# Groups of 16 products in the first idle times of TensorE, and behind the last norm's sum

## The reference

```python
sh1, sc1, g1, sh2, sc2, g2 = _ada(c, ada_w[i], ada_b[i])
hx = _modulate(_rmsnorm(x, norm1_g[i]), sh1, sc1)
csh1, csc1, cg1, csh2, csc2, cg2 = _ada(c_ctx, ada_w[i], ada_b[i])
hc = _modulate(_rmsnorm(ctx, norm1_g[i]), csh1, csc1)
...
return _rmsnorm(x, final_norm_g)
```

## Time and profile before

| | us |
|---|---|
| median of 3 runs | 2122.95 |
| lowest, highest | 2110.27, 2126.66 |
| span of the profiled execution | 2138.7 |

### The profile page before, as it was taken

The page is one execution under the profiler, slowest core; times in us unless marked ns, Lnnn a source line. Parts: engine busy times, 40 slices in busy tenths (PEclk is TensorE's granted clock), DMA queues, the critical chain, the costliest instruction groups (busy, mean ns, idle before and its releaser), DMA issues.

```text
span 2138.7 us, 44829 instructions
## 1 busy us (share of the span) xinstructions
PE 2071.3 (97%) x17120; PEld 1995.6 (93%) x17120; DVE 1608.4 (75%) x1892; ACT 1044.1 (49%) x1489; POOL 81.8 (4%) x63
## 2 busy tenths in 40 slices
PE   6989999999999999999999999999999999999997
PEld 3678888899999999999999989999999999999997
DVE  3238989898888888988888868998886664456665
ACT  2355666545555555433455543465555553335553
POOL 0000000031000000000000211200000000000012
PEclk8999999999999999999999999999999999999999
DMA  9954666796888788899888836968865555555663
GB/s 374 364 218 161 234 219 235 264 379 232 291 293 291 278 291 286 326 371 373 314 293 290 293 110 252 356 217 287 282 233 181 186 185 190 194 194 189 195 189 128
DMA packets 127805, 547.37 MB, mean 256 GB/s; under 512 B 14576, under 2 KB 15088, under 8 KB 107120
## 3 DMA queue, kind: packets, MB, share of 16 engines
q1 hardware_dynamic: 127728, 546.31, 71.9%
HBM read 544.16 MB, written 2.10 MB: 255 GB/s over the span
## 4 chain that ended last, share of the span: by engine, by line
PE 85%; DVE 10%; ACT 2%; DMA 2%; issue 1%; SPq 0%; DVEq 0%; ACTq 0%
PE bank L1397 27%; PE bank L1398 26%; PE bank L1399 26%; DVE acc L878 3%; DVE w_lo L855 2%; DMA early<-early_w 1%; PE bank L1489 1%; PE bank L1476 1%; DVE pt_lo L859 1%; DVE negmax L1054 1%; PE bank L1403 1%; ACT prob L629 1%; PE bank L1405 1%; PE bank L1404 1%; DVE v_lo L859 0%
## 5 line engine op out<-in xcount | busy, mean ns | idle before, releaser
L496 ACT CAST w_hi<-raw 128x1024 fp32r<-128x1024 f32 x642 | 671.9, 1049 | 523.0 <-PE bank L1399 414.9
L855 DVE TENSOR_TENSOR w_lo<-raw,w_hi 128x1024 fp32r<-128x1024 f32 x642 | 787.6, 1239 | 182.8 <-ACT w_hi L496 182.5
L1397 PE MATMUL bank<-h_hi,w_hi 128*128 128x256 f32 x3216 | 899.5, 280 | 3.1 <-DVE h_lo L1182 3.1
L1398 PE MATMUL bank<-h_lo,w_hi 128*128 128x256 f32 x3216 | 898.5, 279 | 0.0
L1399 PE MATMUL bank<-h_hi,w_lo 128*128 128x256 f32 x3216 | 898.4, 279 | 0.0
L1397 PEld LDWEIGHTS bank<-h_hi,w_hi 128*128 128x128 f32 x3216 | 608.7, 189 | 6.1 <-issue 3.7
L1399 PEld LDWEIGHTS bank<-h_hi,w_lo 128*128 128x128 f32 x3216 | 608.4, 189 | 0.0
L1398 PEld LDWEIGHTS bank<-h_lo,w_hi 128*128 128x128 f32 x3216 | 604.3, 188 | 0.0
L1397 PE MATMUL bank<-a_hi,w_hi 128*128 128x256 f32 x1408 | 391.8, 278 | 2.1 <-DVE a_lo L859 2.0
L1399 PE MATMUL bank<-a_hi,w_lo 128*128 128x256 f32 x1408 | 391.2, 278 | 0.0
L1398 PE MATMUL bank<-a_lo,w_hi 128*128 128x256 f32 x1408 | 391.2, 278 | 0.0
(11 more groups left out here) (195 smaller groups left out, 2049.6 us busy)
## 6 DMA issues: line engine op xcount, KB each, us to landing
raw<-weights SPq DMA_DIRECT2D x642, 512.0 KB, 4.8
ada<-ada_late SPq DMA_DIRECT2D x160, 1024.0 KB, 5.1
early<-early_w SPq DMA_DIRECT2D x64, 512.0 KB, 7.9
ctx_s<-ctxT SPq DMA_DIRECT2D x4, 512.0 KB, 5.7
x<-xT SPq DMA_DIRECT2D x4, 512.0 KB, 8.5
outT<-h_pre SPq DMA_DIRECT2D x4, 512.0 KB, 2.6
dft_s<-dft SPq DMA_DIRECT2D x1, 1040.0 KB, 8.3
conv_s<-conv SPq DMA_DIRECT2D x2, 176.0 KB, 5.8
```

Source lines behind the costliest of these rows:

```text
L496: act.copy(w_hi[:, slot, :], raw[:, slot, :]).then_inc(hi_done, 1)
L855: dve.tensor_tensor(w_lo[:, slot, :], raw[:, slot, :], w_hi[:, slot, :].bitcast(f32), ALU.subtract)\
L1397: pe.matmul(out, wh, hi_part, start=first, stop=False)
L1398: pe.matmul(out, wh, lo_part, start=False, stop=False)
```

## The change

ScalarE rounds each piece of x into a slot of `w_hi`, behind its squares, and counts `x_rounded`. TensorE gets three helpers. `run(times, cols)` does 16 products (by default) of 256 columns: a 128x128 piece of slot 2 as stationary operand, a piece of slot 0 as moving one, into `bank[3]`, which nobody reads there. `small(n)` does n float32 products of `ident` with 4 columns and then a `run()`. `short(cols, n)` does n products of so many columns and then a `run()`. They stand behind the pairs a = 0 to 12 of the first quarter, and behind `residual_sum(3)`. No result changes.

```diff
@@ -224,7 +224,7 @@
         sq_done, sqt_done, norm_summed, var_done, std_done, rstd_done = (
             sem(n) for n in ("sq_done", "sqt_done", "norm_summed", "var_done", "std_done", "rstd_done"))
         sq0_done, lat_sq, lat_done, xr_done = sem("sq0_done"), sem("lat_sq"), sem("lat_done"), sem("xr_done")
-        eps_set = sem("eps_set")
+        eps_set, x_rounded = sem("eps_set"), sem("x_rounded")
         pre_done, h_hi_done, h_ready = sem("pre_done"), sem("h_hi_done"), sem("h_ready")
         lat_pre, lat_hi, lat_ready = sem("lat_pre"), sem("lat_hi"), sem("lat_ready")
         kr_taken, kr_rot, kr_step, kr_hi_done, kr_ready, kr_zero = (
@@ -543,6 +543,9 @@
             for n in range(2):
                 for r in range(4):
                     piece_squares(n, r)
+                    if n:
+                        act.copy(w_hi[:, r, :], x[:, QK * r:QK * r + QK, :].rearrange("p k n -> p (k n)"))\
+                            .then_inc(x_rounded, 1)
             std(1, NTOK)
             for g in range(QUARTERS):
                 rows(g)
@@ -1541,6 +1544,22 @@
                     if t % 2:
                         mm.then_inc(chunk_used, 2)
 
+            def run(times=16, cols=SEQ):
+
+                for _ in range(times):
+                    pe.matmul(bank[3][:, 0:cols], w_hi[:, 2, 16:16 + P], w_hi[:, 0, 0:cols], start=True, stop=True)
+
+            def small(n):
+
+                for t in range(n):
+                    pe.matmul(bank[3][:, 4 * t:4 * t + 4], ident, ident[:, 0:P:32], start=True, stop=True)
+                run()
+
+            def short(cols, n=1):
+
+                run(n, cols)
+                run()
+
             def rope_keys(c, half, u0=0, u1=8):
 
                 pe.wait_ge(lo_done, c + 1)
@@ -1561,6 +1580,29 @@
             for a in range(0, N_EARLY, 2):
                 g, k = a // KT, a % KT
                 early_pair(a)
+                if a == 0:
+                    pe.wait_ge(x_rounded, 4)
+                    run()
+                if a == 2:
+                    small(1)
+                    small(2)
+                if a == 4:
+                    small(4)
+                    short(128)
+                if a == 6:
+                    small(8)
+                    short(64)
+                if a == 8:
+                    small(1)
+                    short(32)
+                    short(128, 2)
+                if a == 10:
+                    small(4)
+                    short(128)
+                if a == 12:
+                    small(8)
+                    short(64)
+                    small(2)
                 if g and k == 2:
                     turn(g - 1)
                 if g and 6 <= k < 14:
```

## The result

The changed kernel took 2157.68 us (median of 4, 2146.07 to 2163.23) beside 2118.63 us for the kernel before (4 runs, 2110.27 to 2126.66). The ratio is 1.0157, with a 95% interval of 1.0117 to 1.0198: slower by 33 us, between 25 and 42. The forecast was 21.3 us, with 0.48 each for slower and for within 1%. The direction is right and the size is short by a third. The medians alone are 39 us apart (1.0184, inside the interval), and 2157.68 lies 1.7 us above the forecast range of 2131 to 2156. The ratios here leave out runs that lie more than 1.5% above the fastest of their kernel; medians, lowest and highest stand for all runs. Most of what follows is about why one change can be 33 us in one sample and 21 in the next.

What follows compares the result with a forecast made beforehand. TensorE, with work in 2071.3 of 2138.7 us, was taken as the bound. Front 22.9, give-back -2.6 and tail 1.0 make +21.3 us on 2122.95: 2144 us, 8-in-10 range 2131 to 2156.

Steps and rivals of the forecast that it cites:

- Copies at nothing: ScalarE's four roundings of x at the start add 4.0 us of its time, covered by TensorE's work: price 0.
- 15 runs at 1.83 us, 27.5 us: Groups of 16 products on TensorE ahead of pair a = 14, at full clock, no discount for the repeated operand.
- Small and short products, 8.3 us with the changes between them: In the front: 30 small products 7.5 us, seven short ones 0.6, changes of kind between runs 0.2.
- Changes of kind at the pairs, 2.1 us: In the front: six pairs between float32r products cost 0.3 us more each, two half so 0.3 together.
- Pair a = 14 at 69.1 us: First quarter's pair that sets the whole rest ends at 69.1 us in place of 46.2, 22.9 us later.
- 2.6 us given back: Behind pair a = 14, full clock and loads already landed return 2.6 us, bounds 0 and 5.3.
- Tail 1.0 us: Added products behind the last norm's sum, 12.8 us, end 1.0 us past the last store, bounds 0 and 3.
- the rival's mechanism: Clock falls to half behind each group of eight small products, twice in front, once at the end: 2149 us, chance 0.22.
- Cheaper products: Added products cost less than the profile rows: small ones at half, runs at 107 ns a product: 2137.5 us, chance 0.20.
- Not slower: Up to 190 us the stream of loads sets the pace, so the front's delay comes back: 2121 us, chance 0.05.
- Full give-back: All cold work and both load waits behind 46.2 us leave the path, 5.3 us: 2141.5 us, chance 0.08.
- Every stage from 100 to 2120 us as long as before: Sign of the forecast: past the front, no stage up to 2120 us changes its length.

Runs made afterwards that it cites:

- e5: Kernel before plus only ScalarE's four copies of x and TensorE's wait for them, no added products: 2134.47 us.
- e6: Changed kernel with only the 15 groups of 16 in the front, no small or short products, nothing behind the last sum: 2121.51 us.
- e2: The changed kernel once more, unchanged: 2143.01 us, ratio 1.0099 to the kernel before.
- e8: Changed kernel with only as many added products as the first quarter's waits hold (102), nothing behind the last sum: 2124.68 us, ratio 1.0009 to the kernel before.
- e1: The kernel before, unchanged, measured against itself: 2127.91 us, ratio 1.0011.
- e9: Kernel before plus four 512-column float32 products at two places of each layer's feed-forward: 2115.97 us, ratio 0.9954.
- e11: The kernel of e9 measured once more: 2113.58 us, ratio 0.9976 to the kernel before.
- e4: Changed kernel without the front's added products, keeping the copies and the products behind the last norm's sum: 2123.64 us, ratio 0.9997 to the kernel before.
- e10: Kernel before plus four small 4-column products at the same places as in e9: 2132.82 us, ratio 1.0035.
- e7: Changed kernel with 32 small products in place of eight at three places: 2175.61 us.

## Why the prediction was right, and where it was short

- *Copies at nothing*: right (e5).
- *15 runs at 1.83 us, 27.5 us*: a little low. In the front a step is 117 ns and not 114, so 240 products are 28.1 us (e6).
- *Small and short products, 8.3 us with the changes between them*: 8.1 (e6). *Changes of kind at the pairs, 2.1 us*: about 1.3, what is left of the whole (44.8 - 28.1 - 8.1 - 7.3).
- *Pair a = 14 at 69.1 us*: 67.9. TensorE began 0.8 us sooner, since its clock rose at 11.5 and not at 13.1 us. From the first pair on it is 44.8 us (forecast 45.2). The bet on the whole stretch was right: all of what did not fit into the gap was paid.
- *2.6 us given back*: 2.3 us; the end of pair a = 14 moved by 21.7 and VectorE's 61st instruction by 19.4. That instruction lies 0.6 us apart in before and e1, so the 2.3 is good to about that.
- *Tail 1.0 us*: 0.8 us (1.2 in e2). TensorE ended 12.3 us behind the sum (forecast 12.8).
- *Clock stays full at eight small products*: right; the rival's mechanism is shown at 32.
- *Cheaper products*: fell. *Not slower*: fell; with the DMA share at 0.62 in the front nothing came back. *Full give-back*: fell; e8 has VectorE's turned rows 1.9 us sooner and keeps 0.5 at the 61st instruction.
- *Every stage from 100 to 2120 us as long as before*: this step failed. I took the loops' times of one profile as the kernel's. In the profile of after the shift grew to 26.0 us at 1400 us and fell back to 12.3 behind the last up-projection, in code that was not touched. The steps differ from execution to execution, worth up to 12.6 + 5.0 + 13.0 us in the three loops and 3.4 in layer 1's square product. My own sign of being wrong, a later stage shorter by 10 us or more, came true with it (up 1 by 13.0), though the change is not its cause: e1, without the change, has it too.

So the mechanism and the sum are right, at 19 to 21 us by every measure that takes the draws out. What the 33 us of the result has over it I put down to the draws of four runs beside four; only one of these runs of after has a profile, so that is argued and not shown. My half per cent of scatter in medians was somewhat low (the two medians of after are 14.7 us, 0.7%, apart) and had no cause. Not settled: what decides the draw. With the 512-column products in front of the loops 21 of the 24 runs of e9 and e11 are under 2120 us, where 9 of the 46 runs of before beside them are. Why they help is open, since the step behind such products can also be the long one (e4 above). That a break of another kind does not help (e10) is one kernel and twelve runs.

## What to carry to other kernels

An engine's waits can be filled for nothing only up to their length; the rest is queued in front of the step that everything else waits for, and is paid in full. Before two profiles are compared, look at the count of products in equal stretches of untouched loops. If it differs, subtract the stages and not the spans, or compare the lowest runs. A version with 16 products more (e9, e11) came out at 0.9954 and 0.9976 of the kernel before, the second with 1 inside its interval (up to 1.0003). It makes slow executions rarer and not the fast ones faster: the lowest run of e11 is 2111.63 us, that of before beside it 2104.97.

## What had not been expected of the hardware

TensorE's stream of 128x128 by 256 products has two steps at full clock, 113.3 and 117.8 ns, and keeps the one that it has through a loop of some 2800 products. At a hiccup of 0.05 us it changed in two profiles of the six that have one, and at 863 us it changed, in one direction or the other, in all fourteen profiles. And 32 small products of 4 columns in a row, a TensorE that is busy by the profile, let the granted clock fall to 1.2 GHz 4.3 us after they began. The Trainium skill, "TensorE: Matmul & The Clock Gate", section "Why this matters for your kernels", advises to leave TensorE no long idle gaps between bursts of products. In e7 the clock fell without such a gap: TensorE was busy 1.00 us of every us from 42 to 45.
